# Memory-unit products moved behind a tile's second pointwise unit, in a two-block transformer kernel on one Trainium2 core

## What is computed

```
first_block:   x = x + (silu(h2 @ w_ffn_gate) * (h2 @ w_ffn_up)) @ w_ffn_down
second_block, layer 0:
  h = rmsnorm(x)
  u = h @ w_pw1 + b_pw1                       # the "first pointwise", 1024 -> 2 x 1024
  u = a * sigmoid(gate)
  u = depthwise_conv(u, w_dw, 31 taps) + b_dw
  x = x + silu(layernorm(u)) @ w_pw2 + b_pw2  # the "second pointwise"
  x = x + memory_cross_attention(rmsnorm(x), rmsnorm(mem), w_q, w_k, w_v, w_o)
# k = mem_n @ w_k and v = mem_n @ w_v of both layers depend on the inputs alone
```

## Time and profile before

| | |
|---|---|
| time, median of 3 runs | 2248.03 us (2247.85 to 2248.14) |
| the profiled execution | 2249.73 us, its span 2247.9 us |
| granted clock of TensorE, mean | 0.997 of full speed |
| PE busy | 2216.0 us (99%), 10686 matmuls |
| DVE, ACT, POOL busy | 60%, 43%, 17% |
| last down projection and start of the convolution | 735 to 808 us |
| convolution tiles 1 to 7 | 808 to 952 us |
| tail of the convolution, layernorm | 952 to 988 us |

### The profile page before, as it was taken

One profiled execution on the slowest core, in us unless ns is written; L12 is line 12 of the kernel. 1 busy time (PEld: TensorE's weight loads), 2 busy tenths in 40 slices (PEclk: granted clock), 3 DMA queues, 4 the chain that ended last, 5 costly groups with the idle time before them and its releaser, 6 DMA issues.

```text
span 2247.9 us, 31295 instructions
## 1 busy us (share of the span) xinstructions
PE 2216.0 (99%) x10686; PEld 1802.3 (80%) x10686; DVE 1346.2 (60%) x1910; ACT 971.3 (43%) x1480; POOL 389.6 (17%) x329
## 2 busy tenths in 40 slices
PE   8999999999999999999999999999999999999998
PEld 6777778888888788868888888887777888888887
DVE  5557756654545879965474544576555647454455
ACT  6775645443433566753332222254444333222222
POOL 2231101201010456723040000040001204000003
PEclk9999999999999999999999999999999999999999
DMA  5222223455656756632223333332222222333332
GB/s 150 66 66 63 74 80 94 141 190 189 199 189 199 227 183 211 204 127 80 61 85 103 93 94 103 93 91 66 64 60 66 79 63 84 102 93 95 102 94 86
DMA packets 413080, 253.36 MB, mean 113 GB/s; under 512 B 14832, under 2 KB 394224, under 8 KB 412976
## 3 DMA queue, kind: packets, MB, share of 16 engines
q1 hardware_dynamic: 412080, 249.68, 36.5%
q0 software_dynamic: 896, 2.33, 0.3%
HBM read 232.56 MB, written 18.87 MB: 112 GB/s over the span
## 4 chain that ended last, share of the span: by engine, by line
PE 88%; DVE 4%; ACT 2%; issue 2%; DMA 1%; DVEq 1%; SPq 1%; POOLq 0%; ACTq 0%; POOL 0%
PE bank L1958 25%; PE bank L1960 24%; PE bank L1959 24%; PE bank L1938 2%; PE bank L2431 1%; DVE bank L1661 1%; PE bank L2408 1%; DVE m_w_lo L1267 1%; PE bank L2346 1%; PE bank L2111 1%; PE bank L2336 1%; PE bank L2537 1%; PE bank L2504 1%; PE bank L2249 1%; PE bank L2251 1%
## 5 line engine op out<-in xcount | busy, mean ns | idle before, releaser
L699 ACT ACTIVATE m_w_hi<-m_raw 128x1024 fp32r<-128x1024 f32 x332 | 351.5, 1059 | 826.3 <-PE bank L1960 817.6
L1958 PE MATMUL bank<-m_h_hi,m_w_hi 128*128 128x512 f32 x1504 | 607.1, 404 | 2.5 <-DVE m_w_lo L1267 1.6
L1960 PE MATMUL bank<-m_h_hi,m_w_lo 128*128 128x512 f32 x1504 | 586.9, 390 | 0.0
L1959 PE MATMUL bank<-m_h_lo,m_w_hi 128*128 128x512 f32 x1504 | 586.5, 390 | 0.0
L1267 DVE TENSOR_TENSOR m_w_lo<-m_raw,m_w_hi 128x1024 fp32r<-128x1024 f32 x332 | 448.1, 1350 | 95.2 <-ACT m_w_hi L699 90.4
L1958 PEld LDWEIGHTS bank<-m_h_hi,m_w_hi 128*128 128x128 f32 x1504 | 282.8, 188 | 74.1 <-issue 11.0
L1960 PEld LDWEIGHTS bank<-m_h_hi,m_w_lo 128*128 128x128 f32 x1504 | 282.4, 188 | 60.1
L1959 PEld LDWEIGHTS bank<-m_h_lo,m_w_hi 128*128 128x128 f32 x1504 | 283.1, 188 | 55.2 <-issue 2.2
L1958 PE MATMUL bank<-m_f_hi,m_w_hi 128*128 128x512 f32 x688 | 268.8, 391 | 2.6 <-DVE m_w_lo L1267 2.6
L1960 PE MATMUL bank<-m_f_hi,m_w_lo 128*128 128x512 f32 x688 | 267.8, 389 | 0.0
L1959 PE MATMUL bank<-m_f_lo,m_w_hi 128*128 128x512 f32 x688 | 267.7, 389 | 0.0
(11 more groups left out here) (399 smaller groups left out, 3213.9 us busy)
## 6 DMA issues: line engine op xcount, KB each, us to landing
m_raw<-in_ff_w SPq DMA_DIRECT2D x256, 256.0 KB, 3.0
mem_low<-m_mem_raw_lo SPq DMA_DIRECT2D x32, 512.0 KB, 3.9
m_mem_w_low<-mem_low SPq DMA_DIRECT2D x32, 512.0 KB, 7.4
m_raw<-in_conv_pw_w SPq DMA_DIRECT2D x48, 256.0 KB, 3.1
m_raw<-in_w_in SPq DMA_DIRECT2D x47, 256.0 KB, 3.2
m_raw<-in_w_ffn_gate SPq DMA_DIRECT2D x44, 256.0 KB, 3.3
m_raw<-in_w_ffn_up SPq DMA_DIRECT2D x44, 256.0 KB, 3.2
m_raw<-in_w_ffn_down SPq DMA_DIRECT2D x40, 256.0 KB, 3.0
```

The source lines that it names most:

```text
L699: act.activation(WH[:, v % 2], RAW[:, v % 2], ACT.Copy).then_inc(s.w_hi, 1)
L1958: pe.matmul(o, high[:, r, k, :], hi, start=start, stop=False)
L1959: pe.matmul(o, high[:, r, k, :], lo, start=False, stop=False)
L1960: last = pe.matmul(o, low[:, r, k, :], hi, start=False, stop=stop)
```

## The change

`MEM_SPLIT_AT` was every second MLP unit from 4 to 66; it is now every second one from 2 to 58, and 17, 21 and 41. Unit 59 is the last up projection, and 60 to 67 are the last down projections. On PE all memory units of a tile stand behind its second pointwise unit. On ACT the eviction `mem_out(first)` of a tile's first memory unit moves from the middle of the tile to behind the sigmoid. DVE does 13 of the 19 taps ahead of a tile's first eviction, before it was 10. In the tail, SP loads units 25 to 31 in that order (before 28 and 29 came last), and ACT's high parts of units 29 to 31 stand between the squares, no longer ahead of them.

```diff
-MEM_SPLIT_AT = range(4, 4 + 2 * MEM_UNITS, 2)
+MEM_SPLIT_AT = sorted((*range(2, 60, 2), 17, 21, 41))
@@ SP
-            for i in (25, 26, 27, 30, 31, 28, 29):
+            for i in range(MEM_TAIL, MEM_UNITS):
                 if i == 30:
                     sp.wait_ge(s.unit_done, conv_done)
                 mem_load(i)
@@ ACT, conv_steps
                 for i in range(first + 1, min(last, first + 3)):
                     mem_high(i)
-                mem_out(first)
                 if m > 0:
                     products(m - 1, SUM_TAPS - 4, SUM_TAPS)
                 step(None)
...
                 for i in range(first + 3, last):
                     mem_high(i)
-                for i in range(first + 1, last - 1):
+                for i in range(first, last - 1):
                     mem_out(i)
@@ ACT, the tail
             mem_high(28)
             mem_out(27)
-            for i in range(29, MEM_UNITS):
-                mem_high(i)
             for k in range(KD):
                 act.wait_ge(s.ln_c, k + 1)
                 if k >= 2:
                     act.wait_ge(s.ln_sq_used, k - 1)
                 act.activation((LG, CA)[k % 2][:], CV[:, k, :], ACT.Square).then_inc(s.ln_sq, 1)
+                if k in (2, 4, 6):
+                    mem_high(28 + k // 2)
@@ DVE, conv_steps
-                cut = [0, 10, DVE_TAPS]
+                cut = [0, 13, DVE_TAPS]
@@ PE, conv_units
                 first, last = MEM_TILES[m]
-                mem_product(first)
                 full(HH, HL)
-                for i in range(first + 1, last):
+                for i in range(first, last):
                     mem_product(i)
```

## The result

The changed kernel takes **2252.98 us** (median of 13 runs, 2251.95 to 2254.35), the kernel before 2248.14 us beside it (13 runs, 2247.80 to 2249.32): 0.20% longer, the ratio 1.0020 with a 95% interval from 1.0013 to 1.0027. The forecast was 2246.0, and 2252.98 lies 4.1 us above the upper end of its range.

A forecast was written before the change was run, and what follows sets the result against it. PE, busy 99% of the span, bounds it. Down projection -2.0, to unit 0's end -1.4, to tile 1 +1.9, tile 2 +2.2, tiles 3 to 7 -2.1, tail -0.6: -2.0 us, 2246.0 us (2242.8 to 2248.9).

The forecast's parts named there:

- Splits and start: Last down projection and start of tiles: both low-part waits go, -2.0 us; unit 0 starts at 787.3 without a wait.
- The wait before unit 2: Tile 0: PE waits 5.3 us before unit 2, the clock costs 2.4 more, tile 1 starts 1.5 us sooner.
- Unit 9: Tile 2: PE waits 2.4 us for an eviction behind the sigmoid, and tile 3 starts 0.7 us later.
- rival B: Unit 9's wait in tile 2 also ends at the lower clock, costing 2.9 us more: 2248.9 us; chance 14%.
- DVE's lead keeps the evictions of keys 10, 16 and 22 just ahead of PE: Tiles 3 to 7: only 0.2 us of wait, in tile 3; the last mean comes 1.4 us sooner.
- Tail: After the last mean: squares no longer wait for loads and the three high parts; -0.6 us.
- Sum: All terms from the down projection to the tail together: -2.0 us, giving 2246.0 us from the median.
- the 2.4 us that unit 0 was to win back from the clock: Memory unit 0, tile 0: 2.4 us lost behind the 3.1 us wait, to go with unit 0 at full clock.
- keeps that lead of 2.1 us: From tile 0's `tile_done`, 2.1 us sooner, DVE is full in every tile and stays that much ahead.
- PE waits for keys in tiles 5 and 7: One of the signs, stated beforehand, by which the prediction would be wrong; no size given.

The follow-up runs named there:

- b1: The kernel before with the new `MEM_SPLIT_AT` places and nothing else: 2242.88 us, ratio 0.9976.
- a1: The changed kernel with unit 25's high part moved behind the sigmoid and the two evictions on ACT in the last tile: 2247.99 us, ratio to before 0.9999.
- b4: The kernel before, unchanged, run again for a second profile: 2248.31 us.
- b2: The kernel before with only the tail changed, loads in order of use and the last three high parts between the squares: 2247.53 us, ratio 0.9997.
- b3: The kernel before with the splits' new places and the new tail, the units' order left: 2240.81 us, ratio 0.9969.
- c3: The changed kernel with each tile's first eviction ahead of the sigmoid, unit 25's high part behind the evictions, unit 24's eviction ahead of unit 26's high part: 2239.18 us.

## Why the prediction was wrong, by its steps

- **Splits and start: right.** The first pointwise unit was to start at 775.8 and did at 775.21. Unit 0 starts at 787.49 without a wait and takes 2.87 us at full clock, as forecast (787.3). The three splits in MLP units cost nothing that can be seen: the wait near 740 us, behind all of them, ends at 742.74 before, at 742.43 in the changed kernel and at 742.30 in b1.
- **The wait before unit 2: right**, 4.95 us against 5.3, start 798.21 against 798.3. The clock behind it costs 1.3 us (4.20 us in place of 2.87), not 2.4; in a1 it cost 2.3 (5.13 us), so 2.4 lies at the edge of what the runs show. Tile 1 starts 2.7 us sooner, not 1.5.
- **Unit 9: right in its place and in tile 3's start**, which is +0.7 us as forecast, but by errors that cancel, which is luck: PE came to it 1.0 us sooner (842.1, not 843.1), the wait was 2.15 against 2.4, and the lower clock came behind it, as rival B said, and took 1.6 us (unit 9 4.20 us against 2.84 at full clock in a1, and the pointwise units behind it 11.11 against 10.88). It ate the 1.2 us won at tile 1.
- **"DVE's lead keeps the evictions of keys 10, 16 and 22 just ahead of PE": the step that failed.** Keys 10 and 16 held to 0.4 us, and tile 7 starts 0.96 us sooner. Key 22 did not hold. PE was ready for unit 24 by 946.9 us, and ACT's eviction of unit 22, which frees the bank, came at 950.95. I had looked only at DVE, and taken the eviction to follow the sigmoid by the gate's time. The list of tile 7 has one entry that no other tile has, unit 25's high part ahead of the sigmoid, and its load depends on unit 22, which the change had moved. Unit 22's end at 943.9 and the load's 5.1 us from its second issue to the high part give 949.4, the same sum as for unit 3. It cost 4.02 us of wait and 1.5 of clock (4.35 us for unit 24), and a1 measures it: 5.0 us. With it the last mean is 3.9 us late instead of 1.4 early.
- **Tail: right in sign, too small.** From the last mean to unit 29 it gained 1.3 us, not 0.6.
- **Sum.** Forecast -2.0 in the profile, measured +2.6: of the 4.6 between them, 5.3 are at the last mean, and the tail gave 0.7 back. The further 2.3 us between the medians are where the two profiled executions lay among their runs. I took a difference in the one for a difference in the other, and that was worth 2 us of error by itself. One term shows how: the 2.4 us that unit 0 was to win back from the clock were 1.6 in the second profile of before (b4) and 0.1 in b2's, with the same program up to there.
- **That DVE "keeps that lead of 2.1 us" is no limit on what arrives.** In the changed kernel it held: ACT's products of tile 0 started 2.7 us sooner (804.65 against 807.36) and DVE's first `tile_done` 3.1 us sooner (823.81 against 826.89). But the lead follows the start of the tiles, and b1's forecast, 2 to 3 us, missed that: in b1 the same two steps and tile 1 all come 5.7 to 5.8 us sooner than in b4, and 6.1 us arrive at the last mean. The splits are worth 5.2 us, and I hid that by summing them with the order that took it away again. With the move of the memory units as a term of its own, against splits and tail alone, its two forecast waits (5.3 and 2.4 us) would have stood there as its price.

My own condition, "PE waits for keys in tiles 5 and 7", is what happened (0.37 and 4.02 us).

## What to carry to other kernels

When work moves later on one engine, list every buffer that it frees, and follow each load that waits for one to the engine that takes it in: whatever stands behind that entry in the list is late too. Do this for every iteration whose list differs from the others, first and last above all. The remedy was to put the short eviction ahead of the entry that waits, or that entry behind it: a few lines for 12.9 us. And cost each part of a change by itself, against the kernel with the other parts: splits and tail alone (b3) give 7.3 of the 9.3 us of the fastest version (c3). The Trainium skill's page "PSUM — Partial Sum Buffer", section "Engine vs sequencer instructions", says that ScalarE's queue is "strict FIFO"; the trace agrees, with the 0.36 us eviction of unit 0 behind a part that waited 5.90 us for its load.

## What the runs showed of the hardware

**The same wait is followed by a different clock.** Unit 0 waits 3.13, 3.14 and 3.14 us in the two profiles of before and in b2, where the program up to there is the same, and takes 5.29, 4.47 and 2.97 us to the second pointwise unit. The windows of b4 and of b2 behind the wait:

```profile
788.00:790.00 2.00, 2.00 (x11) 2.00 (x11) 1.38 (x2) 2.00 (x3) 0.00 (x0) 0.50 0.00 0
790.00:792.00 2.00, 2.00 (x15) 2.00 (x14) 0.00 (x0) 0.01 (x1) 0.00 (x0) 0.71 0.67 200
```

```profile
788.00:790.00 2.00, 2.00 (x20) 2.00 (x19) 1.40 (x2) 2.00 (x3) 0.00 (x0) 1.00 0.00 0
790.00:792.00 2.00, 2.00 (x14) 1.75 (x13) 0.00 (x0) 0.42 (x2) 0.00 (x0) 1.00 0.69 205
```

Behind 2.15 us unit 9 ran partly at half clock in two profiles (4.20 and 4.00 us) and at full clock in a1 (2.84). Behind the tail's 1.95 us, which I took for safe, the clock fell in b1, and the squares with their exchange took 8.76 us (964.52 to 973.28) instead of 7.14:

```profile
964.52 1.90 PE L2391 MATMUL bank<-m_ln_sq,m_con 128*128 128x512 f32 x2 [1.95 <-ACT m_ln_sq L1100]
966.22 1.91 PE L2391 MATMUL bank<-m_conv_a,m_con 128*128 128x512 f32 x2
```

Between 735 and 1000 us the ten waits of 4 us and more, in six profiles, all had a fall behind them; waits of 1.83 us and less had none. A single trace therefore doesn't say what a wait of 2 to 3 us costs: in these traces it was 0 to 2.4 us on top of itself. What decides between them stays open. The Trainium skill's page "TensorE: Matmul & The Clock Gate", section "Part 1: The HAM clock gate", says of the slow stretch at a kernel's start that "it's run-variable", with a different number of slow matmuls in runs of one kernel. The three lengths of unit 0 show the same in the middle of a kernel, behind a wait. The forecast read one trace as a rule, no loss behind 1.95 and a loss behind 3.1, and that gave rival B too small a chance.
